# Pooled projections copied out of PSUM by ScalarE, and a value product split over both column halves of TensorE

## The reference

```python
h = _rms(x, attn_norm_g)
proj = h @ w_in                      # q, k, v, gates, pool_in, merge_logits
o = gate_c * o_cmp + gate_s * o_slc + gate_w * o_swa     # 16 heads of 64, 4 key/value groups
attn_branch = einsum("bshd,hde->bshe", o, w_head_out)
pooled = _multiscale_pool(pool_in)   # 4 groups of 256 channels, means over 2, 4, 8, 16 tokens
pool_branch = einsum("bsgc,gce->bsge", pooled, w_pool) * pool_scale
merge = sigmoid(merge_logits)
y = merge[0] * attn_branch + merge[1] * pool_branch
x = x + y @ w_out
```

## Time and profile before

| | |
|---|---|
| median of 3 runs | 3329.18 us |
| the runs | 3334.08, 3326.02, 3329.18 us |
| time of the profiled execution | 3327.28 us |
| its span, first to last instruction | 3325.5 us |
| granted TensorE clock, mean | 0.994 |
| TensorE busy | 3230.0 us, 97% |
| VectorE, ScalarE, GpSimd busy | 1893.6, 1495.2, 181.5 us |
| chain that ended last: TensorE, VectorE, ScalarE, DMA | 80%, 9%, 4%, 3% |

### The profile page before, as it was taken

The page is one execution under the profiler, slowest core; times in us unless marked ns, Lnnn a source line. Parts: engine busy times, 40 slices in busy tenths (PEclk is TensorE's granted clock), DMA queues, the critical chain, the costliest instruction groups (busy, mean ns, idle before and its releaser), DMA issues.

```text
span 3325.5 us, 59687 instructions
## 1 busy us (share of the span) xinstructions
PE 3230.0 (97%) x25865; PEld 3126.3 (94%) x25865; DVE 1893.6 (57%) x1716; ACT 1495.2 (45%) x1560; POOL 181.5 (5%) x163
## 2 busy tenths in 40 slices
PE   7999999999999999999999999999999999999998
PEld 6988889899879999999999999999988999999998
DVE  6754555666777655554444545555676555555454
ACT  4344444465564664443333434443455444434342
POOL 1140000000011210100000000100000000000001
PEclk9999999999999999999999999999999999999999
DMA  6653445588874445555555555555444666666664
GB/s 210 189 165 115 130 124 157 181 284 283 278 252 146 147 154 176 175 177 177 173 176 174 174 176 177 177 173 176 153 127 131 193 196 190 194 196 192 191 195 144
DMA packets 554463, 598.37 MB, mean 180 GB/s; under 512 B 11792, under 2 KB 533264, under 8 KB 554288
## 3 DMA queue, kind: packets, MB, share of 16 engines
q1 hardware_dynamic: 550240, 588.42, 56.1%
q0 software_dynamic: 1552, 5.92, 0.6%
q10 hardware_dynamic: 2496, 1.43, 0.2%
HBM read 593.63 MB, written 2.10 MB: 179 GB/s over the span
## 4 chain that ended last, share of the span: by engine, by line
PE 80%; DVE 9%; ACT 4%; DMA 3%; issue 2%; SPq 1%; POOL 1%; ACTq 0%; DVEq 0%; POOLq 0%
PE acc L582 22%; PE acc L580 22%; PE acc L578 22%; DVE low L1791 3%; ACT high L1249 2%; PE psx L1095 1%; PE acc L997 1%; PE acc L999 1%; PE acc L998 1%; DMA raw<-in_w_expert_gate 1%; ACT probs L1380 1%; PE acc L1080 1%; PE psx L1080 1%; PE psx L824 1%; PE acc L1078 1%
## 5 line engine op out<-in xcount | busy, mean ns | idle before, releaser
L578 PE MATMUL acc<-gh,high 128*128 128x256 f32 (+1 forms) x4416 | 902.6, 286 | 29.1 <-DVE low L1791 25.3
L582 PE MATMUL acc<-gh,low 128*128 128x256 f32 (+1 forms) x4416 | 892.0, 283 | 0.0
L580 PE MATMUL acc<-gl,high 128*128 128x256 f32 (+1 forms) x4416 | 892.0, 284 | 0.0
L1791 DVE TENSOR_TENSOR low<-raw,high 128x2048 fp32r<-128x2048 f32 x263 | 609.0, 2320 | 427.6 <-ACT high L1249 427.0
L2052 DVE TENSOR_TENSOR low<-raw,high 128x2048 fp32r<-128x2048 f32 x264 | 605.2, 2292 | 378.2 <-ACT high L1446 378.2
L578 PEld LDWEIGHTS acc<-gh,high 128*128 128x128 f32 x4416 | 688.3, 189 | 39.3 <-issue 22.9
L1446 ACT ACTIVATE high<-raw 128x2048 fp32r<-128x2048 f32 x264 | 505.4, 1914 | 488.3 <-DMA raw<-in_mlp_w 481.6
L582 PEld LDWEIGHTS acc<-gh,low 128*128 128x128 f32 x4416 | 684.3, 190 | 0.0
L580 PEld LDWEIGHTS acc<-gl,high 128*128 128x128 f32 x4416 | 677.6, 189 | 0.0
L1249 ACT ACTIVATE high<-raw 128x2048 fp32r<-128x2048 f32 x263 | 502.3, 1913 | 340.0 <-DMA raw<-in_w_kv 67.8
L582 PE MATMUL acc<-fh,low 128*128 128x272 f32 (+1 forms) x2048 | 411.5, 282 | 0.0
(11 more groups left out here) (442 smaller groups left out, 3581.5 us busy)
## 6 DMA issues: line engine op xcount, KB each, us to landing
raw<-in_mlp_w SPq DMA_DIRECT2D x256, 1024.0 KB, 5.3
raw<-in_w_in SPq DMA_DIRECT2D x60, 1024.0 KB, 5.3
raw<-in_a_w_in SPq DMA_DIRECT2D x40, 1024.0 KB, 5.1
raw<-in_w_expert_up SPq DMA_DIRECT2D x32, 1024.0 KB, 6.5
raw<-in_w_expert_down SPq DMA_DIRECT2D x32, 1024.0 KB, 5.1
raw<-in_w_kv SPq DMA_DIRECT2D x32, 1024.0 KB, 5.4
raw<-in_w_expert_gate SPq DMA_DIRECT2D x28, 1024.0 KB, 6.0
raw<-in_a_w_out SPq DMA_DIRECT2D x20, 1024.0 KB, 4.9
```

The source lines that it names most:

```text
L578: pe.matmul(o[n], hw[:, k, c[n]], h, start=first, stop=False)
L580: pe.matmul(o[n], hw[:, k, c[n]], l, start=False, stop=False)
L582: m = pe.matmul(o[n], lw[:, k, c[n]], h, start=False, stop=last)
L1791: dve.tensor_tensor(tile(low, u, slot), tile(raw, u, slot), tile(high, u, slot).bitcast(F32), ALU.subtract)\
```

## The change

There are two edits. The eight pairs of pooled projections leave PSUM on ScalarE, with a Copy that has `pool_scale` as its scale, and not on VectorE. They stand in ScalarE's order at places of their own: pairs 0 to 3 behind `high` of unit 30, then the last window's `ph`, pairs 4 and 5, `high` of unit 31, pairs 6 and 7. VectorE's order is now the third window's `pl`, `low` of unit 30, the last window's `pl`, `low` of unit 31, and then the first maxima.

The value product of the compressed branch (b = 2) is now two products of 256 columns, the first into partitions 0 to 63 and columns 0 to 255, the second into partitions 64 to 127 and columns 256 to 511. Since the halves are added later, the sum is the same. One semaphore increment follows the second.

```diff
--- before.py
+++ after.py
@@ -820,8 +820,13 @@
                 pe.wait_ge(pt_out, n + 1)
                 if j == 0 and n:
                     pe.wait_ge(o_out, 2 * g + i)
-                side = slice(HD, P) if b == 1 else slice(0, HD)
-                m = pe.matmul(psx[side, 3, :], v, pts[0:K, n % 2, :], start=j < 2, stop=j == (NT[i] - 1 if b != 1 else NT[i] - 2))
+                if b == 2:
+                    for k, side in enumerate((slice(0, HD), slice(HD, P))):
+                        m = pe.matmul(psx[side, 3, 256 * k:256 * k + 256], v, pts[0:K, n % 2, 256 * k:256 * k + 256],
+                                      start=False, stop=True)
+                else:
+                    m = pe.matmul(psx[slice(0, HD) if b == 0 else slice(HD, P), 3, :], v, pts[0:K, n % 2, :],
+                                  start=j < 2, stop=False)
                 m.then_inc(o_mm, 1)
 
             def heads_out(g):
@@ -1343,6 +1348,20 @@
                 act.wait_ge(pooled, n + 1)
                 act.activation(ph[:, 2 * g:2 * g + 2, :], pw[:, 0, :, :], ACT.Copy).then_inc(pooled_hi, 1)
 
+            def project_out(x):
+                j, q = x // 4, x % 4
+                b = B0["wpool"] + x
+                if q == 3:
+                    act.wait_ge(unit_done, U0["wpool"] + j + 1)
+                else:
+                    act.wait_ge(wp_half, 3 * j + q + 1)
+                if x == 0:
+                    act.wait_ge(acc_free, B0["wpool"])
+                for k in range(2):
+                    t = 4 * POOL_ORDER[2 * j + q // 2] + 2 * (q % 2) + k
+                    m = act.activation(pb[:, t, :], acc[:, 2 * (b % 2) + k, 0:S], ACT.Copy, scale=col("pool_scale", t))
+                m.then_inc(acc_free, 1)
+
             def rope_tables():
                 act.wait_ge(angle_ready, 1)
                 act.activation(ropes[:, :], angle[:, 2, :], ACT.Sin)
@@ -1361,7 +1380,11 @@
             after.setdefault(23, []).append(kc_take)
             after.setdefault(24, []).append(kc_root)
             for n, u in enumerate((24, 26, 27, 28)):
+                if n == 3:
+                    after.setdefault(u, []).extend([lambda x=x: project_out(x) for x in range(4)])
                 after.setdefault(u, []).append(lambda n=n: pool_hi(n))
+            after[28].extend([lambda: project_out(4), lambda: project_out(5)])
+            after[29] = [lambda: project_out(6), lambda: project_out(7)]
             for u in range(30):
                 hi_c(u + 2)
                 for f in after.get(u, []):
@@ -1957,18 +1980,8 @@
             pool_low(2)
             for j in range(2):
                 lo_c(U0["wpool"] + j + 2)
-                for q in range(4):
-                    b = B0["wpool"] + 4 * j + q
-                    if j == 0 and q == 2:
-                        pool_low(3)
-                    if q == 3:
-                        dve.wait_ge(unit_done, U0["wpool"] + j + 1)
-                    else:
-                        dve.wait_ge(wp_half, 3 * j + q + 1)
-                    for k in range(2):
-                        t = 4 * POOL_ORDER[2 * j + q // 2] + 2 * (q % 2) + k
-                        m = dve.tensor_scalar(pb[:, t, :], acc[:, 2 * (b % 2) + k, 0:S], col("pool_scale", t), None, ALU.mult)
-                    m.then_inc(acc_free, 1)
+                if j == 0:
+                    pool_low(3)
 
             def maxima(g, i, r0):
```

## The result

The changed kernel takes 3324.74 us (median of 12 runs, 3320.56 to 3330.37), the kernel before 3331.39 us in the same series (12 runs, 3326.02 to 3339.59). The ratio is 0.998, with a 95% interval of 0.9973 to 0.9988: 6.65 us less (4 to 9 us by the interval). The interval excludes no change, but it does not exclude a gain under 0.2%, so the kernel is faster and the change still counts as one within 0.2%. The forecast was 5.9 us less, with a change within 0.2% as the likelier outcome.

What follows compares the result with a forecast made beforehand. The prediction took TensorE, busy for 97% of the span, as the bound. Copies 4.6, clock -0.75 and split 2.1 made 5.9 us, taken from 3329.2 to forecast 3323.3 us, range 3318 to 3328.

Steps and rivals of the forecast that it cites:

- The copies: Pooled projections: ScalarE copies take 0.84 us a pair, the first stall falls from 4.24 to 1.85 us, 4.6 us remain gained.
- The chain behind `high` of unit 31: ScalarE's `high`, VectorE's `low`, then first maxima: 4.6 us early, 1.1 less than TensorE's 5.7.
- The split: Compressed branch's value product, made eight times: 1.00 us becomes 0.63, saving 0.37 each, of which 2.1 us pass in all.
- My own bound for products that don't run side by side: Split value product: four passes of 0.315 us, 1.26 us, a loss of 0.26 each.
- The clock: Half-clock spells on TensorE after the new stalls and waits: 0.75 us lost, bounds 0 and 1.5.
- the 1.85 us stall: TensorE's first stall in the pooled projections, near 215 us: no half-clock loss counted, clock at 1.00 behind it.
- the wait at 245: TensorE waiting for the weighted probabilities: 2.5 us instead of 1.41, with 0.75 us of half-clock loss counted.
- the forecast's own price: One drop to half clock on TensorE costs about 1.5 us.
- a sign of being wrong: Across the kernel: the forecast is wrong if half-clock spells differ in number by more than one.

Runs made afterwards that it cites:

- experiment 3: Changed kernel with both 256-column products of the compressed branch put in the same column half; 3326.02 us, ratio 0.9988 to the kernel before.
- experiment 6: Changed kernel with the unread filler products before the transposes raised from 16 to 36 or 18; 3322.08 us, ratio 0.9973 to the kernel before.
- Experiment 5: Changed kernel with the copies of pair 5 done by VectorE before `low` of unit 31, not by ScalarE; 3325.19 us, ratio 0.9981 to the kernel before.
- experiment 1: Kernel before with only the pooled-projection copies moved to ScalarE, the value product left whole; 3328.37 us, ratio 0.9995 to the kernel before.
- experiment 7: Changed kernel with 14 filler products in the first stall of the pooled projections; 3324.16 us, ratio 0.9979 to the kernel before.

## Why the prediction came out right

**The copies.** Forecast 0.84 us a pair and a stall of 1.85 us; measured 0.84 and 1.87. Without a half-clock spell scores came after 13.4 us and maxima after 15.55 (experiments 3 and 6), where the forecast has 12.9 and 15.3. The maxima are thus 4.3 us early, not 4.6. The pace of 0.118 us for a while behind the stall in experiments 3 and 6, which the forecast took as 0.113, is part of the rest.

**The chain behind `high` of unit 31.** The forecast let 1.1 us of TensorE's gain be lost to it and expected a wait of 2.5 us for the weights; it was 2.36 (1.74 in experiment 3, where TensorE itself kept the slower pace). Experiment 5 took the cause away, and the wait went back to 1.41.

**The split.** The size was off: 0.57 us and not 0.63, so 0.43 saved each, 3.4 in all. Of these 2.4 us pass (forecast 2.1): the idle 0.20 us before the maxima of 296.75 is used up, and behind the last product nothing passes, since the wait for `yh` grew from 2.34 us to 2.76. But the sum is better than its parts. From one first transposes to the next, experiment 6 is shorter than experiment 1 by 0.40, 0.20, 0.28, 0.53, 0.23, 0.52 and 0.21 us, where the forecast has 0.37 and 0.20 in turn. After the first group most passes where little was expected, and the other way round; no run says why. The rule of the Trainium skill (TensorE: Matmul & The Clock Gate, "Part 3: Packing small matmuls — row/col tiling"), by which a weight load overlaps a running product only in another row group, spoke against the split. The trace does not agree with it: both halves use the same 15 rows, the product got shorter, from 1.00 to 0.57 us, and it did not when both products were put in one half. The weight loads show it too. All four of the split product fall in the 0.19 us from 294.52, while its products run until 295.10; with both products in one half the four take 0.62 us (first row: changed kernel; second: experiment 3):

```profile
294.52 0.19 PEld L825 LDWEIGHTS psx<-pts,vcT 15*64 15x64 f32 x4
```

```profile
291.80 0.62 PEld L825 LDWEIGHTS psx<-pts,vcT 15*64 15x64 f32 x4
```

My own bound for products that don't run side by side, 1.26 us, was wrong too: experiment 3 shows 1.01.

**The clock.** This is the step in which the forecast was weakest. It booked no spell for the 1.85 us stall and half a spell for the wait at 245. In the changed kernel's profile there was a spell behind both: products stay at half pace until 218.8, and two stretches, behind the waits at 245.43 and 485.20, show it too:

```profile
247.00:249.00 2.00, 2.00 (x11) 2.00 (x11) 0.53 (x1) 2.00 (x3) 0.00 (x0) 0.50 0.00 0
...
486.00:488.00 2.00, 2.00 (x11) 2.00 (x10) 0.69 (x1) 2.00 (x2) 0.00 (x0) 0.50 0.00 0
```

Over the profiles, none of the five waits of 1.41 to 1.74 us before the first transposes was followed by half clock, two of the five stalls of 1.78 to 1.89 us were, and 26 of the 35 waits of 2.12 to 2.65 us. The same wait can go either way: 2.37 us before 246.47 in experiment 1 was not followed, 2.36 us in the changed kernel and in experiment 7 was. By the forecast's own price, half a spell for the stall and half for the wait make 1.5 us and not 0.75. With 4.3 and 2.4 the sum is then 5.2 us; with no loss at all it is 6.7. The measured 6.65 has an interval of 4 to 9 us and can't tell the two apart, so the number says nothing for this term.

The forecast named as a sign of being wrong that the spells differ in number by more than one. From the first projection to `yh` the two profiles have three (behind 219.13, 283.57 and 420.23) and six, so by the profiles alone the sign was there. The timed runs don't bear it out. A spell like that behind 219.13 takes about 0.0005 off the mean clock of a run (an estimate: half of 3.12 us in 3325), three more would take off 0.0015, and the means are 0.9916 after and 0.9912 before, with standard errors of 0.0003 and 0.0001. So on average the change brought no further spells; the profile of before was an execution with few of them. The level was helped by chance: the forecast started from 3329.18 us, three runs that lay 2.2 us below the later median of twelve, and was short by 0.75 us on the gain, so the time came out 1.4 us from the measured one.

**What stays open.** The shares of the two parts in the totals, 1.7 and 2.7 us by their ratios with intervals of 3 us to each side, are not settled by the timed runs; the distances say 4.3 and 2.4. Nor is it settled what decides in one execution whether a wait of about 2 us is followed by a spell. In the four profiles with the split and 16 fillers before the transposes all 18 of the waits of 2.12 to 2.65 us were, in the four without it 8 of 17. Whether the split itself brings spells on is open; the mean clock of the timed runs with the split alone, 0.9915, shows no loss against 0.9912.

## What to carry to other kernels

When an engine frees a buffer late, look first at what stands ahead of the copy in its own order: here moving the copy ahead of a subtraction that could wait brought the scores and maxima as early as moving it to an idle engine did. If it is moved, price what it now stands ahead of on the new engine, and follow that chain to the next wait, which is where the gain is cashed. Two products with 64 output rows each, written to different halves of the partitions, ran here in the time of one. Where a later step adds the two halves anyway, as `heads_out` does, such a product can be split by its columns. Here 1.00 us became 0.57, and of the 3.4 us saved in eight products 2.4 reached the end of the stage.

## What was unexpected of the hardware

A product of 512 columns and two products of 256 columns in the same half took the same time, 1.00 and 1.01 us: there was no price for the second weight load. And waits of 2.12 to 2.65 us cost TensorE time twice, by their length and, in 26 of 35 cases, by half clock behind them: fillers cannot shorten the chain that TensorE waits for, yet with them the stretch from the first transposes to `yh` took 6.6 us less in the profile, and the median was 2.7 us lower, though the intervals overlap.
